# x loaded by ScalarE's queue and turned by halves, x parked sooner, products of ones in TensorE's waits, and the last map's first tile applied alone

## The reference, cut to what matters

```python
# block 1, once for each of two layers
u = rmsnorm(x, norm_mix[l]);  proj = u @ w_in[l]           # attention, convolution, gates
x = x + merged @ w_mix_out[l]
u = rmsnorm(x, norm_mlp[l]);  x = x + square(relu(u @ w_mlp_up[l])) @ w_mlp_down[l]
x = rmsnorm(x, norm_final)                                 # between the blocks
# block 2
h = modulate(rms_norm(x, norm1_g), shift1, scale1);  proj = h @ w_in_2
x = x + gate1 * (mixed @ w_out_2)
h2 = modulate(rms_norm(x, norm2_g), shift2, scale2)
# peer(h2): h2 @ w_query -> scores against sub_keys -> 16 best experts a head, softmax g
#   z = h2 . u_experts[idx];  a = gelu(z) * g;  y = sum a * v_experts[idx]
x = x + gate2 * peer(h2);  return rms_norm(x, final_g)
```

## Time and profile before

| | |
|---|---|
| time, median of 3 executions | 1780.56 us (1779.72 to 1785.5) |
| the profiled execution's own time | 1784.67 us |
| its span, first to last instruction | 1783.4 us |
| mean granted TensorE clock | 0.992 |
| PE busy | 1722.5 us, 97% |
| DVE busy | 1350.0 us, 76% |
| ACT busy | 916.9 us, 51% |
| POOL busy | 63.9 us, 4% |
| chain that ended last | PE 77%, DVE 15%, issue 3%, DMA 2%, ACT 2% |
| bytes moved | 333.36 MB, mean 187 GB/s |

### The profile page before, as it was taken

The page is one execution under the profiler, slowest core; times in us unless marked ns, Lnnn a source line. Parts: engine busy times, 40 slices in busy tenths (PEclk is TensorE's granted clock), DMA queues, the critical chain, the costliest instruction groups (busy, mean ns, idle before and its releaser), DMA issues.

```text
span 1783.4 us, 33286 instructions
## 1 busy us (share of the span) xinstructions
PE 1722.5 (97%) x11642; PEld 1580.5 (89%) x11642; DVE 1350.0 (76%) x2380; ACT 916.9 (51%) x1610; POOL 63.9 (4%) x116
## 2 busy tenths in 40 slices
PE   8999999999999999989979999999999999999997
PEld 7999899989999879979869999999999988888885
DVE  6976788878976678878674999987888766666665
ACT  4345544444454434456544455567777645455453
POOL 0000011000000122100000000000000000000000
PEclk9999999999999999999999999999999999999999
DMA  5655598754445699753335355553443355555553
GB/s 199 211 186 198 171 344 272 251 189 154 154 154 166 233 331 293 251 166 130 118 110 186 130 188 177 182 172 135 139 141 131 131 188 190 196 191 193 195 189 140
DMA packets 91612, 333.36 MB, mean 187 GB/s; under 512 B 11001, under 2 KB 11177, under 8 KB 91074
## 3 DMA queue, kind: packets, MB, share of 16 engines
q1 hardware_dynamic: 79634, 288.54, 48.3%
q0 software_dynamic: 10912, 39.38, 6.6%
q10 hardware_dynamic: 976, 4.19, 0.6%
HBM read 329.93 MB, written 6.07 MB: 188 GB/s over the span
## 4 chain that ended last, share of the span: by engine, by line
PE 77%; DVE 15%; issue 3%; DMA 2%; ACT 2%; POOL 0%; DVEq 0%; ACTq 0%; SPq 0%; POOLq 0%
PE bank L207 23%; PE bank L208 23%; PE bank L209 23%; DVE Z L86 6%; DVE w_lo L184 4%; PE bank L1690 3%; PE bank L270 1%; DMA raw<-stream 1%; ACT w_hi L179 1%; DMA gate<-w_ada 1%; DVE yc L86 1%; DVE x L86 1%; PE bank L477 1%; PE bank L1276 1%; PE bank L770 1%
## 5 line engine op out<-in xcount | busy, mean ns | idle before, releaser
L184 DVE TENSOR_TENSOR w_lo<-raw,w_hi 128x1024 fp32r<-128x1024 f32 x546 | 661.9, 1222 | 173.8 <-ACT w_hi L179 172.6
L179 ACT ACTIVATE w_hi<-raw 128x1024 fp32r<-128x1024 f32 x546 | 574.0, 1053 | 277.1 <-PE bank L209 189.6
L207 PE MATMUL bank<-u_hi,w_hi 128*128 128x256 f32 x2416 | 700.0, 290 | 9.2 <-ACT Z L86 3.9
L209 PE MATMUL bank<-u_hi,w_lo 128*128 128x256 f32 x2416 | 685.7, 284 | 0.0
L208 PE MATMUL bank<-u_lo,w_hi 128*128 128x256 f32 x2416 | 685.6, 284 | 0.0
L207 PEld LDWEIGHTS bank<-u_hi,w_hi 128*128 128x128 f32 x2416 | 465.5, 193 | 22.9 <-issue 8.9
L208 PEld LDWEIGHTS bank<-u_lo,w_hi 128*128 128x128 f32 x2416 | 465.3, 193 | 4.6 <-issue 2.4
L209 PEld LDWEIGHTS bank<-u_hi,w_lo 128*128 128x128 f32 x2416 | 464.9, 192 | 0.0
L207 PE MATMUL bank<-w_hi,a_hi 128*128 128x512 f32 x768 | 301.0, 392 | 4.2 <-DVE a_lo L963 1.8
L208 PE MATMUL bank<-w_lo,a_hi 128*128 128x512 f32 x768 | 300.0, 391 | 0.0
L209 PE MATMUL bank<-w_hi,a_lo 128*128 128x512 f32 x768 | 299.3, 390 | 0.0
(11 more groups left out here) (270 smaller groups left out, 1657.0 us busy)
## 6 DMA issues: line engine op xcount, KB each, us to landing
raw<-stream SPq DMA_DIRECT2D x546, 512.0 KB, 3.3
gate<-w_ada POOLq DMA_DIRECT2D x48, 512.0 KB, 6.5
space<-b_ada POOLq DMA_DIRECT2D x6, 512.0 KB, 7.0
t_rows<-t_by_distance POOLq DMA_DIRECT2D x8, 256.0 KB, 4.1
rpb_rows<-rpb_pad POOLq DMA_DIRECT2D x8, 224.0 KB, 3.8
gains<-gains POOLq DMA_DIRECT2D x3, 512.0 KB, 5.1
bias_a<-t_rows POOLq DMA_DIRECT2D x1, 1536.0 KB, 11.4
bias_b<-rpb_rows POOLq DMA_DIRECT2D x16, 96.0 KB, 7.9
```

The costliest lines, as they stand in the source:

```text
L179: nc.scalar.activation(w_hi[:, s, :], raw[:, s, :], ACT.Copy).then_inc(s_hi, 1)
L184: nc.vector.tensor_tensor(w_lo[:, s, :], raw[:, s, :], w_hi[:, s, :].bitcast(F32), ALU.subtract).then_inc(s_split, 1)
L207: M.matmul(o, lh, rh, start=start, stop=False, skip_group_check=True)
L209: return M.matmul(o, ll, rh, start=False, stop=stop, skip_group_check=True)
```

## The change

Five edits are made together.

- The two loads of x are issued by ScalarE's queue. SP issues the gain row, `kept` and piece 0, and then waits until x's second tile has landed before it issues pieces 1 to 3. GpSimd waits for the same before its first load.
- DVE multiplies the first halves of both tiles, then the second halves; the first halves are turned, piece 0's `w_hi` is made, the second halves are turned, and `u_lo` of the first halves, piece 0's `w_lo` and `u_lo` of the second halves follow on DVE.
- `keep_clock(b, n)` issues n matmuls of 128x512 whose two operands are one fp32r column of ones, broadcast. They write bank b, and nobody reads the result. Three stand ahead of the spreading of the gain, 28 at the start of block 2, 24 at its second norm, and 7 after the last map.
- The store of x is issued after `squares` of the second tile, ahead of the roots.
- The last map is applied in two parts: expert tile 0 first, which lets `weighted(0)` go, and tiles 1 to 127 after it, ahead of `weighted(1)`.

```diff
--- before.py
+++ after.py
@@ -262,6 +262,12 @@
         def take(i):
             PE.wait(*free.get(i, ()))
 
+        def keep_clock(b, n):
+
+            for _ in range(n):
+                M.matmul(bank[b][:, :], one_r[:, 0:1].to_broadcast([P, P]), one_r[:, 0:1].to_broadcast([P, 512]),
+                         start=True, stop=True, skip_group_check=True)
+
         def transposes(b, sources, marks):
 
             take(b)
@@ -538,10 +544,11 @@
 
         gain_row = cc[0:1, :, :].rearrange("p a n -> p (a n)")
         nc.sync.dma_start(gain_row, gains1[0:1, :]).then_inc(s_gain0, 16)
-        nc.sync.dma_start(x[:, 0, :], x_in[0:P, :]).then_inc(s_x[0], 16)
         nc.sync.dma_start(kept[:, :], kept_in).then_inc(s_kept, 16)
+        for tt in range(NT):
+            nc.scalar.dma_start(x[:, tt, :], x_in[tt * P:(tt + 1) * P, :]).then_inc(s_x[tt], 16)
         load_first(0)
-        nc.sync.dma_start(x[:, 1, :], x_in[P:2 * P, :]).then_inc(s_x[1], 16)
+        nc.sync.wait_ge(s_x[1], 16)
         for s in range(1, RING):
             load_first(s)
 
@@ -561,6 +568,7 @@
         hot = buf["p"][0:DH, 0:2, :].rearrange("p a n -> p (a n)")
         t5 = buf["p"][0:DH, 2, 0:H]
         t5_row = buf["p"][0:H, 3:5, :].rearrange("p a n -> p (a n)")
+        G.wait_ge(s_x[1], 16)
         G.dma_start(hot, t5_hot).then_inc(s_t5, 16)
         G.dma_start(t5, t5_in).then_inc(s_t5, 16)
         G.dma_start(c_col, c_cols).then_inc(s_c, 16)
@@ -626,25 +634,29 @@
         space_junk = work[:, :, :].rearrange("p a n -> p (a n)")
         u_ready = [[(), ()], [(), ()]]
         ones = VE.go((), V.memset, one[:, :], 1.0)
-        VE.go((ones,), V.tensor_copy, one_r[:, :], one[:, :])
-        PE.wait(ones, (s_gain0, 16))
+        ones = VE.go((ones,), V.tensor_copy, one_r[:, :], one[:, :])
+        PE.wait(ones)
+        keep_clock(4, 3)
+        PE.wait((s_gain0, 16))
         for n in range(2):
             i = M.matmul(bank[2 + n][:, :], one[0:1, 0:1].to_broadcast([1, P]), gain_row[:, n * 512:(n + 1) * 512],
                          start=True, stop=True)
         spread = PE.done(i)
+        gained = [[None, None], [None, None]]
+        for n in range(2):
+            for tt in range(NT):
+                cols = slice(n * 512, (n + 1) * 512)
+                gained[tt][n] = VE.go((spread, x_marks[tt][n]), V.tensor_tensor, xn[:, tt, cols], x[:, tt, cols],
+                                      bank[2 + n][:, :], ALU.mult)
+            free[2 + n] = (gained[0][n], gained[1][n])
         for tt in range(NT):
-            for n in range(2):
-                cols = slice(n * 512, (n + 1) * 512)
-                m = VE.go((spread, x_marks[tt][n]), V.tensor_tensor, xn[:, tt, cols], x[:, tt, cols], bank[2 + n][:, :],
-                          ALU.mult)
-                free[2 + n] = (m,)
-                turn_chunk(tt, n, m, u_ready)
-                if n:
-                    lower_next()
-                if n and not tt:
-                    lower_next()
-                    split(0)
-        lower_next()
+            turn_chunk(tt, 0, gained[tt][0], u_ready)
+        split_hi(0)
+        for tt in range(NT):
+            turn_chunk(tt, 1, gained[tt][1], u_ready)
+        lower_next(), lower_next()
+        split_lo(0)
+        lower_next(), lower_next()
         u_ready = by_feature(u_ready)
         for c in range(1, AHEAD):
             split(c)
@@ -1181,6 +1193,8 @@
             return junk_mark[0]
 
         splits = held_pieces(*last_downs, sums())
+        take(5)
+        keep_clock(5, 28)
         m = VE.go((g_marks[1][1],), V.scalar_tensor_tensor, space_lo[1], xn[:, 1, 512:], 1.0, xn[:, 1, 512:],
                   ALU.mult, ALU.mult, accum_out=st[:, 8, 1:2])
         VE.wait(m, junk_mark[0])
@@ -1454,7 +1468,10 @@
                              [[bank[4][:, :], bank[6][:, :]], [bank[0][:, :], bank[1][:, :]]], branch_sums(), whole=True, ahead=False)
         split_hi(splits[0]), split_hi(splits[1])
         split_lo(splits[0])
+        take(5)
+        keep_clock(5, 24)
         m = squares(x, space_lo[0], 5, x_marks, 1)
+        S.dma_start(x_dram.rearrange("t p d -> p t d"), x[:, :, :]).then_inc(s_park, 16)
         split_hi(splits[2])
         m = token_roots(m)
         m1 = AC.go((m, *x_marks[1]), S.activation, xn[:, 1, :], x[:, 1, :], ACT.Copy, scale=st[:, 3, 1:2])
@@ -1462,8 +1479,6 @@
         split_lo(splits[1])
         h2_ready = modulated_to_u(xn, (m, m1), scaled, 1)
         split_lo(splits[2])
-        AC.wait(x_marks[NT - 1][1])
-        S.dma_start(x_dram.rearrange("t p d -> p t d"), x[:, :, :]).then_inc(s_park, 16)
 
         ph1.close()
         Z = sb(ctx, "Z", [P, PK * T])
@@ -1751,9 +1766,18 @@
             mapped = g + 1
         assert mapped == groups
         times_kept(PK - 1, kept_before)
-        for g in range(applied, groups):
+        for g in range(applied, groups - 1):
             apply(g, PK)
-
+        M.wait_ge(s_z, PK + 1)
+        keep_clock(4, 7)
+
+        def apply_last(tiles):
+            V.wait_ge(s_g, groups)
+            zt = by_tile[:, tiles, tokens(groups - 1)]
+            V.tensor_tensor(zt, zt, map_of(groups - 1, tiles), ALU.mult).then_inc(s_m, 1)
+
+        V.wait_ge(s_z, PK + 2)
+        apply_last(slice(0, 1))
         S.wait_ge(s_m, groups)
         S.wait_ge(s_mu, steps - 1)
 
@@ -1781,6 +1805,8 @@
 
         acc = [[bank[0][:, :], bank[1][:, :]], [bank[2][:, :], bank[3][:, :]]]
         weighted(0, 0, None)
+        apply_last(slice(1, PK))
+        S.wait_ge(s_m, groups + 1)
         for j in range(RING):
             expert_down(j % 2, j, first=j == 0)
         quads, piece = at["quads"], at["piece"]
```

## The result

The changed kernel takes 1770.97 us in the median of 6 executions (1768.55 to 1773.41), the kernel before 1782.36 us in 6 on the same chip (1779.72 to 1785.5). The ratio is 0.9939, with a 95% interval of 0.9927 to 0.995. That is 11.4 us less, where 11.8 us were forecast, and the time lies in the range of 1764 to 1775 us around the forecast 1768.8. The profiled executions are 13.4 us apart (1784.67 and 1771.3 us); the paragraph on the sum comes back to the 2 us between these two differences.

A forecast was written before the change was run, and what follows sets the result against it. TensorE was taken as the bound, so time is won only where it idles or runs at half clock. Gains of 2.7 + 1.65 + 5.6 + 1.85 = 11.8 us from 1780.56 gave 1768.8 us, range 1764 to 1775.

The forecast's parts named there:

- The start: Start of the kernel: PE's first product at about 12.25 instead of 14.96, a gain of 2.7 us.
- The cost of 0.25 us: Start: three fillers delay the end of the gain's spreading from 6.10 to 6.35, hidden by x's landing.
- the same 25 slow matmuls: Start, first product: the clock rises after the same 25 matmuls as before.
- with the clock up early ... still nothing: Start, piece 3's `w_lo`: done by 20.3, wanted by PE at about 23, or 20.9 with early clock; cost nothing.
- Rival 3: Start: fillers raise the clock before the first product, 14.3 us gained in all, 1766.3 us; chance 0.12.
- Hidden costs: Start: `cw_all` lands near 19, DVE waits for it instead of reading at 18.2; no cost to PE.
- Block 2's start: Start of block 2: 28 fillers halve the transposes' time, first `hT` 0.5 us sooner; gain 1.65 us, from 0 to 1.7.
- The second norm: Block 2's second norm: restart 4.1 us sooner, clock kept up for 1.55 us; together 5.6 us, from 2.3 to 5.7.
- The last map: Last map: split apply and seven fillers keep the clock up; gain 1.85 us, from 0.3 to 2.0.
- the first (the clock falls behind the transposes): Block 2: clock falls in or behind the transposes despite fillers; 8.4 us gained in all, 1772.2 us; chance 0.15.
- The second (x late): Start: x's second tile lands as late as before, start loses 0.8; 8.3 us in all, 1772.3 us; chance 0.12.
- The fourth (dear fillers): Fillers cost more than 0.227 us each, delaying PE's real work; 1808 us at fp32 matmul price; chance 0.03.

The follow-up runs named there:

- the old last map: Changed kernel with the last map applied in one go and without the seven fillers behind it: median 1771.43 us.
- the kernel with the old order: Changed kernel with its new loads and all fillers, but the start's old tile-by-tile, half-by-half order, piece 0 split between the tiles: median 1775.06 us.
- the kernel with 56 fillers: Changed kernel with 56 fillers instead of 28 at the start of block 2: median 1777.27 us.
- the 52 transposes: Changed kernel with 52 and 45 transposes of the identity in place of block 2's 28 and 24 fillers: median 1772.17 us.
- banks 2 and 3: Changed kernel with query tiles from the third on in banks 2 and 3, and eight fillers ahead of the last output piece's second half: median 1770.46 us.

## Why the prediction was right, and where its steps were off

**The start: 2.7 us forecast, 2.8 us in place, 3.2 us on the mean with the clock.** The first product came at 12.16 against the 12.25 of the working. The cost of 0.25 us that the working gave to the three fillers was the gain row's. The second tile landed by 6.9 (POOL's first load, which waits for it, was issued at 6.94), sooner than the 7.6 taken. What I took as the same 25 slow matmuls was wrong in five of eleven profiles: there they are fast. With M1 at 15.1 to 15.25 in five profiles of the new order and at 16.7 to 17.4 in six, a mean of 16.2, against 19.8 in the two of the kernel before, the gain is 3.6 us on the mean and 5.1 at best at this mark. But the prediction's "with the clock up early ... still nothing" for what stands behind it was wrong. In the five profiles with an early clock PE reaches `score` before DVE has made it and is idle for 0.65 us, at 21.7; in the other six there is no such wait, and the same matmul starts at 22.4 to 23.1. Set against the profile of the old last map, whose first product came at 12.16 too, the changed kernel is 2.0 us ahead at M1 and 1.1 us behind these matmuls; the 0.9 us lie in M1-M2. At this matmul the new order is 3.2 us ahead on the mean (22.3 against 25.6) and 4.4 at best. Rival 3 thus happened in five of eleven profiles, with 1.1 us left of its 2.5, and not through its mechanism: the kernel without the three fillers shows it too. The reason given for the part was also incomplete. I had worked x's landing into the sum; the kernel with the old order shows that the landing alone is worth nothing. The order on DVE moved the first product, and by the landing times it could do so only because x was there.

**Hidden costs.** `cw_all` landed 5.6 us after its issue at 9.77, at 15.4, and DVE read it at 15.49 without an idle time before it. I had reckoned with 19, and with a wait that nobody would see. In two of the other profiles DVE did wait for it, 0.75 and 0.86 us, and then for ACT in any case. The two lines, from the list of DMA issues and from DVE's timeline:

```profile
cw_all<-conv_w POOLq DMA_DIRECT2D x1, 12.0 KB, 5.6
...
15.49 0.17 DVE L86 COPY cw<-cw_all 128x12 f32<-128x12 f32 x1
```

**Block 2's start: 1.65 us forecast, 1.4 to 1.7 us measured** (M2-M3, 98.63 and 98.97 against 97.25). The fillers, the halved transposes and the first `hT` 0.47 us sooner (0.66 us after the transposes' start, 1.13 before) came as worked out. The wait moved to the ladder: PE has a new short idle time of 0.40 us, at 795.06, until the first `u_lo` is there.

**The second norm: 5.6 us forecast, 5.3 us measured** (M4-M5). Counted from the transposes, the restart won 3.9 us, not 4.1 (934.19 - 920.43 = 13.76 before, 924.19 - 914.30 = 9.89 after): PE needed 1.08 us after the last `u_lo` for the six matmuls, the semaphore and the drain, where I had put 0.7, and then waited 1.40 us, not 1.6. The clock's part is the rest of the 5.3, 1.5 us, as forecast. The experiments split it: the place of the store is 4 us against the kernel before if the fillers are out, and 5.6 us if they are in; the fillers here are 1.0 to 1.6 us. The two edits share the loss of the clock, so their single worths don't add up.

**The last map: 1.85 us forecast, 1.9 us in the profiles, but only 0.4 us of it without the clock.** The fault is in what the fillers got credit for. The seven fillers were not seen to do anything: the clock stayed up in both profiles without them, and even in one with the old wait of 1.78 us. That the part came out at 1.9 us is luck as far as the 1.5 us of the clock go: they were won against two profiles in which it fell, and the runs without the fillers kept the clock as well.

**The sum.** By stretches, on the mean: 3.2 + 1.5 + 5.3 + 0.4 to 1.9 = 10.4 to 11.9 us; the medians say 11.4 and 9.2. A forecast within 0.4 us of the first of them is closer than the working deserves. The 13.4 us between the two profiled executions hold a start that was at its worst before and at its best after. M1-M2 differs by up to 2.9 us between the profiles (775.20 to 778.10, leaving out the kernel with 56 fillers, whose extra ones lie in it). The same program has 777.25 and 775.20 in one case, 777.58 and 776.44 in the other, so it isn't the edits, but for the early clock's 0.9 us. Most of it lies in its last 200 us: from the last four transposes ahead of block 1's last MLP (at 599.01 before, at 594.70 in the changed kernel) to M2 it takes 195.8 to 199.1 us. What makes it longer there is open. ScalarE waits for pieces of the stream in 620:680, 31.6 us in 16 waits before and 26.9 us in 15 after, but these two profiles have nearly the same M1-M2. This stretch and the clock are about as large as the 5 us between executions of one kernel.

The rivals: the first (the clock falls behind the transposes) is refuted by the two rows of fillers. One thing that I had read against it was wrong, that the start at 934.19 "stays slow" from the beginning: PE had stood idle for 3.92 us with a granted clock of 1.00 in 930:934, its first seven matmuls are 0.12 us apart, and only then the clock falls, until 938.5:

```profile
934.42 0.28 PE L208 MATMUL bank<-u_lo,w_hi 128*128 128x256 f32 x1
...
935.28 0.42 PE L209 MATMUL bank<-u_hi,w_lo 128*128 128x256 f32 x1
```

So this start does not show that transposes help to bring the clock up; the rows of fillers and the 52 transposes are what speaks. The second (x late) happened in one of twelve profiles, for 0.75 us. The fourth (dear fillers) is refuted by 0.225 us each, and the kernel with 56 shows what it would have looked like.

**What stays open.** The new order with the old loads was not tried; that it would win nothing is an estimate from landing times. Whether the seven fillers ever save anything would need more profiles than two. The medians put the change at 11.4 and at 9.2 us on two occasions, and both intervals exclude no change; which of them is nearer is not settled.

## What to carry to other kernels

A store or load that only guards the reuse of a buffer belongs where its data is final, ahead of the work that doesn't need it: here 4 to 5.6 us for one moved line. Fill a wait of PE only if it is long (6 us here), and keep the row shorter than the wait: a filler that outlasts it is paid in full. Waits of 1.8 to 2 us cost the clock in some profiles and not in others, so a single profile can't tell what a filler is worth there. When an early landing is bought, look at who reads the data and whether that engine was free to read it; here the landing alone won nothing. And follow a gain to the next place where the engine waits for another: of the early clock's 2.0 us 0.9 were gone 7 us later.

## What the runs showed of the hardware that I had not expected

- The same program comes to full clock at different moments. With the new order the first product's matmuls change from 0.21 to 0.12 us apart at 12.4 or at 15.7 to 16.9; in the kernel before at 18.4 and 20.4.
- The same idle time can end with a full or a half clock. After 2.03 us of waiting the clock fell in four of thirteen profiles; after 1.78 us in two of three; after 1.3 to 1.4 us in none. Length alone doesn't decide: waits of 1.95 and 2.25 us near 628 (the old last map; banks 2 and 3) left it at 1.00. The Trainium skill, "TensorE: Matmul & The Clock Gate", Part 1, says that the monitor that watches TensorE's activity runs freely and does not start afresh with a kernel; the different moments in one and the same program agree with it.
- The clock can fall after the wait is over, with PE at work again: 0.9 us after the restart behind 3.92 us of idle time (934.19), and 1.2 us after it behind 2.87 us in the kernel with transposes as fillers (628.93; granted clock 1.00 in 628:630, 0.52 in 630:633). Whoever looks at the first matmuls behind a wait alone calls them safe.
- Transposes of fp32 keep a full clock up by themselves: 52 in 5.84 us, with 16 in 1.94 us behind them.
